# Output projection to feed-forward: new weight layout and order at the seam, and parts 2, 3, 3, 3 of the first down product

## The chip, the cores and the metric

The kernel runs on one core of a Trainium2 chip. Its engines are TensorE (PE: matmuls into the accumulator memory PSUM), VectorE (DVE), ScalarE (ACT) and GpSimd (POOL) for elementwise work, and SyncE (SP), whose queue issues all DMAs here. The on-chip memory is SBUF. The metric is the time of one execution on the device in microseconds, as the median of several runs.

## The reference

One encoder layer is applied to two sequences of 1024 tokens and 1024 channels, all in float32:

```python
h = rms_norm(x, ln_mix_pre); z = h @ w_in            # -> pool group | q | k | v
mix = jnp.concatenate([pool_out, attn_out], axis=-1) @ w_out
x = x + rms_norm(mix, ln_mix_post)
h = rms_norm(x, ln_ffn_pre)
f = (jax.nn.silu(h @ w_gate) * (h @ w_up)) @ w_down  # 1024 -> 2816 -> 1024
x = x + rms_norm(f, ln_ffn_post)
e = p @ w_ple_proj
g = jax.nn.sigmoid(x @ w_ple_gate + b_ple_gate)
return x + e * g
```

The change touches what lies between `@ w_out` and the first products of the feed-forward, and the order of the parts of `@ w_down` for the first sequence.

## The kernel before

A float32 product is done as three products of a rounded part ("hi") and a rest ("lo"): hi x hi, hi x lo, lo x hi. The hi of each operand is a copy on ScalarE, the lo a subtraction on VectorE. This making of two parts is called a split here.

**Output projection.** The mixed channels of 16 tiles of 128 tokens are multiplied by `w_out` (8 strips of 128 rows, split and resident in `wout_0` to `wout_3`, two strips in each). For each tile n: SP loads the mixed channels (`mixed_in`), ScalarE and VectorE split them into `ct` (`concat_hi`, `concat_lo`), TensorE multiplies two column halves one after the other (`mix_half`), 24 matmuls each. Then `post_a` (norm, gain, residual, giving `x1`), `turn_back` (TensorE transposes x1), `x1_out` (ScalarE copies it out of PSUM), `post_b` and `turn_scale` (the second norm's scale, transposed), GpSimd's gain (`xg`), and `h2_out` on VectorE, which writes `h2a` for an even and `h2b` for an odd tile. For each pair of tiles GpSimd makes four more operands from these (`forms_made`), and SP stores seven forms in memory (`store_forms`), and each tile's x1 (`store`).

**Feed-forward.** It is a blocked product of Strassen's kind: 7 products instead of 8 for a block of 2 x 2. A *unit* is one block of output; it has 7 *steps*, and step i multiplies form i of the activations (resident in `reg[:, k, i]`, k up to 4) with form i of the weights, which pass through the three places of `ring`. Steps are counted by `st`; UNITS holds all of them. Gate and up: 11 units j per sequence, nk = 4, that is 24 matmuls of 128 x 512 a step. Down: the inner dimension of 22 blocks is 11 pairs, cut into four parts by `DPART`; each part has two units q, and a step has 6 x nk matmuls: 18 for nk = 3, 12 for nk = 2. Parts after the first are added to `acc` (on VectorE and, for three of four blocks, on GpSimd: `add_base`). The last part's results leave through `ev` to `f_turned`.

Around each step, in the code's order: `weights_hi(st + 2)` on ScalarE, `weights_lo(st + 2)` on VectorE, the weight sums on GpSimd (`sums`), and the accumulations out of PSUM on VectorE (`g_tile`, `c22_middle`, `c22_end`, `c11_end`, `c12_end`, `c21_end`). Every engine works through its list strictly in order. TensorE's step st waits for `w_split` (the lo of its weights) and, in the first unit on new forms, for the form: for a gate product `op_split`, for a down product `op_in`.

**Filling `reg`.** The forms of a down part are loaded straight into `reg` (`fill_in`), form i when the last unit before has done its step i. For a gate product (`f` = 0 for sequence 0, 5 for sequence 1) 14 pieces of 1024 elements, two for each form, go through six places (three of `stg`, three of `fhi`): SP loads (`piece_in`), ScalarE copies (`fill_hi`), VectorE subtracts (`fill_lo`), and the place is free again (`stg_free`). For sequence 1 this is done in steps 3 to 6 of the last down unit and 0 to 2 of the next.

`reg` lies over the memory of the output projection (`wout`, `h2a`, `h2b`, `x1t`, `x1`, `xs_d`, `mixn`, `forms`). So a fill waits until what lay there is read: in `fill_hi` forms 0 to 3 wait for `mix_done` of the last tile, form 4 for the stores of even pairs, 5 and 6 for those of all pairs and of x1:

```python
elif i < 4:
    act.wait_ge(S["mix_done"], 2 * NSEQ * NT)
else:
    act.wait_ge(S["h2_st0"], 32 * NP * NSEQ)
    if i >= 5:
        act.wait_ge(S["h2_st1"], 32 * NP * NSEQ)
```

The order at the seam is that of the code: on TensorE lines L1332 to L1368, on SP the loop over n that ends in the pieces, on ScalarE and VectorE the loop over tiles, then `post_a(15)` and the fills, then the loop over steps.

Of the kernel before, what the change touches and what calls it, by code (L numbers as in the profile page):

```python
# [55 lines left out]
DPART = (3, 3, 3, 2)  # L56
DPART0 = (0, 3, 6, 9)
# [20 lines left out]
LASTP = len(DPART) - 1  # L78
# [110 lines left out]
def encoder_layer(nc, x, xt, p, ident_d, cos_d, sin_d, edge_d, g_mix_pre, g_mix_post, w_in, pool_w,  # L189
# [12 lines left out]
    with top:  # L202
# [26 lines left out]
        def stage_end(e):  # L229
# [65 lines left out]
        wout_0 = sb(s_d, "wout_0", [P, 2, 2, D], F32R)  # L295
        h2a = sb(s_d, "h2a", [P, 2, KT, P])
        x1t = sb(s_d, "x1t", [P, KT, P])
        wout_1 = sb(s_d, "wout_1", [P, 2, 2, D], F32R)
        h2b = sb(s_d, "h2b", [P, 2, KT, P])
        x1 = sb(s_d, "x1", [P, D])  # L300
        wout_2 = sb(s_d, "wout_2", [P, 2, 2, D], F32R)
        xs_d = sb(s_d, "xs_d", [P, 2, D])
        mixn = sb(s_d, "mixn", [P, D])
        wout_3 = sb(s_d, "wout_3", [P, 2, 2, D], F32R)
# [3 lines left out]
        gpost = sb(s_d, "gpost", [P, D])  # L308
        sb(s_d, "ws_ring_d", [P, 2 * 2 * CH + 3 * 4 * CH])
        ct_1 = sb(s_d, "ct_1", [P, 2, KT, P], F32R)  # L310
        gffn = sb(s_d, "gffn", [P, KT])
        rows_r = sb(s_d, "rows_r", [P, P])
        sb(s_d, "gffn_rest", [P, D - KT - P])
        junk_d = sb(s_d, "junk_d", [P, D], BF16)
        sb(s_d, "stg_d", [P, 3 * 2 * CH])
        xg = sb(s_d, "xg", [P, KT, P])
        s_d.close()
        wout, ct = (wout_0, wout_1, wout_2, wout_3), (ct_0, ct_1)
# [65 lines left out]
            "x1_sum", "x1_scale", "x1_root", "h2_ready", "x1_turned", "x1_out", "h2_turned", "h2_out", "x1_stored",  # L384
# [90 lines left out]
        def _(sp):  # L475
# [140 lines left out]
            def weights_in(u, m):  # L616
# [43 lines left out]
            def piece_in(f, q):  # L660
# [123 lines left out]

            for n in range(NSEQ * NT):
# [1666 lines left out]
```

## Time and profile before

| what | value |
|---|---|
| median of 3 runs | 2411.22 us (2408.73 to 2412.57) |
| profiled execution | 2405.9 us |
| its span | 2404.1 us |
| PE busy | 2332.2 us (97%) |
| DVE busy | 1688.6 us (70%) |
| ACT busy | 1046.8 us (44%) |
| POOL busy | 929.3 us (39%) |
| granted TensorE clock, mean | 0.989 |
| DMA | 394.30 MB, mean 164 GB/s |

Shares are of the span. A busy PE is not one at its peak, since the ends of its pipelined matmuls are modelled: what counts is the distance between starts. Idle time of an engine other than PE costs something only where PE ends up waiting for it. In rows of the trace the releaser of a wait stands behind `<-`, with the tile that it wrote and its line.

### The profile page before, as it was taken

The numbers are of one execution on the slowest core, as the hardware profiler recorded it, in microseconds if no ns is written. First come the engines' busy times: TensorE is split into PE (matmuls) and PEld (weight loads), VectorE is DVE, ScalarE is ACT, GpSimd is POOL, SyncE is SP. The second block draws the span as 40 slices with busy tenths as digits, with TensorE's granted clock in tenths as the row PEclk, the third lists the DMA queues.
The fourth block names the chain that finished last, engine by engine and source line by source line (L and its number), as shares of the span: only waits on it lengthen the run. The fifth ranks groups of instructions, "written<-read, shape, count | busy, mean of one in ns | idle before, by whom it ended". The sixth has DMA issues, their size and how long they took to land.

```text
span 2404.1 us, 29814 instructions
## 1 busy us (share of the span) xinstructions
PE 2332.2 (97%) x11120; PEld 1933.1 (80%) x11120; DVE 1688.6 (70%) x1785; ACT 1046.8 (44%) x1554; POOL 929.3 (39%) x557
## 2 busy tenths in 40 slices
PE   8999999999999979999999999899999999999999
PEld 7888788888777867888888888688788888877877
DVE  5756888888744667767666556888888866565752
ACT  4433788888743444333333222444433333233321
POOL 0000335444314554444444365454446634550210
PEclk9999999999999989999999999999999999999999
DMA  5222211100058785535447766655457596677431
GB/s 196 74 78 87 84 40 36 40 31 32 24 149 236 208 244 161 169 125 171 149 154 304 277 237 199 220 184 192 158 189 246 202 349 254 238 248 241 147 116 75
DMA packets 315103, 394.30 MB, mean 164 GB/s; under 512 B 18513, under 2 KB 222161, under 8 KB 314833
## 3 DMA queue, kind: packets, MB, share of 16 engines
q1 hardware_dynamic: 314960, 392.40, 48.4%
q8 instruction: 90, 1.47, 0.3%
q14 instruction: 53, 0.43, 0.1%
HBM read 254.99 MB, written 137.36 MB: 163 GB/s over the span
## 4 chain that ended last, share of the span: by engine, by line
PE 84%; DVE 8%; issue 3%; DMA 2%; ACT 2%; SPq 1%; POOL 1%; DVEq 0%; POOLq 0%; ACTq 0%
PE ps L1348 45%; PE ps L1126 32%; PE ps L1129 7%; DVE reg L2092 2%; DVE ring L2084 1%; DMA xb<-x_turned 1%; SPq L632 1%; DMA f_turned<-ev 1%; DVE fb L2393 0%; POOL fb L1120 0%; DVE x2l L2224 0%; DVE fhi L2203 0%; DVE rnorm L2390 0%; SPq L614 0%; DMA stg<-mix_turned 0%
## 5 line engine op out<-in xcount | busy, mean ns | idle before, releaser
L1348 PE MATMUL ps<-reg,ring 128*128 128x512 f32 x5544 | 1271.9, 392 | 28.7 <-DVE ring L2084 20.9
L1348 PEld LDWEIGHTS ps<-reg,ring 128*128 128x128 f32 x5544 | 1046.8, 189 | 253.2 <-DVE ring L2084 26.1
L1448 ACT ACTIVATE ring<-wraw 128x1024 fp32r<-128x1024 f32 (+2 forms) x152 | 143.7, 946 | 385.5 <-PE ps L1348 382.1
L2084 DVE TENSOR_TENSOR ring<-wraw,ring 128x1024 fp32r<-128x1024 f32 (+2 forms) x152 | 231.3, 1523 | 64.2 <-ACT ring L1448 63.3
L1126 PE MATMUL ps<-win,ht 128*128 128x512 f32 (+1 forms) x1152 | 227.2, 358 | 10.2 <-DVE win L1929 10.0
L1126 PEld LDWEIGHTS ps<-win,ht 128*128 128x128 f32 x1152 | 190.6, 191 | 40.6 <-issue 10.6
L1448 ACT ACTIVATE ring<-ws 128x1024 fp32r<-128x1024 f32 (+2 forms) x114 | 107.9, 947 | 237.0 <-PE ps L1348 228.7
L2028 DVE TENSOR_TENSOR pt<-ps,pt 128x512 fp32r<-128x512 f32 x256 | 173.0, 687 | 46.5 <-ACT pt L1448 42.3
L2084 DVE TENSOR_TENSOR ring<-ws,ring 128x1024 fp32r<-128x1024 f32 (+2 forms) x114 | 176.8, 1551 | 40.3 <-ACT ring L1448 39.1
L1126 PE MATMUL ps<-wout,ct 128*128 128x512 f32 x768 | 185.4, 401 | 7.0 <-DVE ct L2040 7.0
L1448 ACT ACTIVATE pt<-ps 128x512 fp32r<-128x512 f32 x256 | 153.7, 601 | 62.7 <-PE ps L1129 59.3
L1126 PEld LDWEIGHTS ps<-wout,ct 128*128 128x128 f32 x768 | 145.9, 193 | 38.3 <-DVE ct L2040 7.6
L1033 POOL TENSOR_TENSOR ws<-wraw,ws 128x1024 f32<-128x1024 f32 (+2 forms) x38 | 83.5, 2198 | 208.8 <-DMA wraw<-in_w_up 110.8
L1993 DVE TENSOR_REDUCE negmax<-ps 128x1 f32<-128x1024 f32 x128 | 156.0, 1219 | 9.8 <-PE ps L1126 8.6
L1129 PEld LDWEIGHTS ps<-ident,prob 128*128 128x128 f32 x1024 | 125.7, 140 | 42.5 <-issue 11.0
L1129 PE MATMUL ps<-ident,prob 128*128 128x128 f32 x1024 | 153.5, 272 | 2.4 <-DVE pt L2028 2.2
L1126 PE MATMUL ps<-keys,qs 128*128 128x512 f32 x512 | 150.8, 417 | 1.1 <-ACT prob L1564 1.1
L1126 PE MATMUL ps<-pt,values 128*128 128x512 f32 x512 | 149.8, 415 | 0.0
L1064 POOL TENSOR_TENSOR acc<-acc,ev 128x1024 f32<-128x1024 f32 x36 | 106.4, 2957 | 102.8 <-DVE ev L2104 102.8
L1564 ACT ACTIVATE prob<-ps,negmax 128x1024 f32<-128x1024 f32 x128 | 142.7, 1115 | 1.6 <-DVE negmax L1993 1.6
L1039 POOL TENSOR_TENSOR ws<-wraw,ws 128x1024 f32<-128x1024 f32 (+2 forms) x38 | 104.5, 2749 | 52.9 <-DVE ring L2084 52.9
L1027 POOL TENSOR_TENSOR ws<-wraw 128x1024 f32<-128x1024 f32 (+2 forms) x38 | 100.3, 2639 | 46.0 <-DVE ring L2084 46.0
(209 smaller groups left out, 2959.3 us busy)
## 6 DMA issues: line engine op xcount, KB each, us to landing
reg<-ff_forms SPq DMA_DIRECT2D x42, 1536.0 KB, 10.1
ff_forms<-fhi SPq DMA_DIRECT2D x88, 512.0 KB, 3.2
wraw<-in_w_gate SPq DMA_DIRECT2D x88, 256.0 KB, 4.2
wraw<-in_w_up SPq DMA_DIRECT2D x88, 256.0 KB, 4.6
ff_forms<-ev SPq DMA_DIRECT2D x44, 512.0 KB, 2.9
wraw<-in_w_down SPq DMA_DIRECT2D x48, 384.0 KB, 5.7
reg<-ff_forms SPq DMA_DIRECT2D x14, 1024.0 KB, 5.9
xt_a<-in_xt SPq DMA_DIRECT2D x16, 512.0 KB, 4.5
```

Of the source, the lines that this page charges most:

```text
L1027: ins = nc.gpsimd.tensor_tensor(s0, raw_block(u, 0, 0), raw_block(u, 1, 0), ALU.subtract)
L1033: ins = nc.gpsimd.tensor_tensor(s1, raw_block(u, 1, 1), s0, ALU.subtract)
L1039: ins = nc.gpsimd.tensor_tensor(s1, raw_block(u, 0, 1), s1, ALU.subtract)
L1064: nc.gpsimd.tensor_tensor(t, t, ev[:, 0], ALU.add).then_inc(S["acc_sum"], 1)
L1126: return nc.tensor.matmul(out, lhs, rhs, start=start, stop=stop)
L1129: return nc.tensor.transpose(out, src, ident[:])
L1348: last = nc.tensor.matmul(ps[:, 2 * chain + m, :], ring[:, st % 3, a, m, k * P:(k + 1) * P], reg[:, k, i, e, :], start=OPENS[i] and k == 0 ...
L1448: copy = lambda out, src, **k: nc.scalar.activation(out, src, ACT.Copy, **k)
L1564: nc.scalar.activation(prob[:, s % 2, :], pair(2 * (s % 2)), ACT.Exp, bias=negmax[:, s:s + 1], scale=1.0, accum_out=rowsum[:, s:s + 1]).th ...
L1993: V.tensor_reduce(negmax[:, s:s + 1], pair(2 * (s % 2)), AX.X, ALU.max, negate=True)\
L2028: V.tensor_tensor(pt[at][:, 1], ps[:, 4 + half, :].rearrange("p (k n) -> p k n", k=4), f(pt[at][:, 0]), ALU.subtract).then_inc(S["p_split" ...
L2084: V.tensor_tensor(ring_block(u, st, 1), weight_source(u, i), f(ring_block(u, st, 0)), ALU.subtract).then_inc(S["w_split"], 1)
```

## The change

1. `w_out` is laid by form: hi and lo of the strips are placed so that, after strips 3, 4 and 6 of the last tile, the memory of forms 0, 1 and 2 is free (`w_out_at`, semaphore `wout_free`). `gpost`, `gffn` and `rows_r` move, so that the place of piece 5 is free early.
2. TensorE runs the last tile strip by strip, both halves in each strip; `turn_scale(13)` stands after strip 3 and `turn_back(14)` after strip 5. Step 0 of the feed-forward follows at once, with `turn_scale(14)` in it, then `turn_back(15)`, step 1 with `turn_scale(15)`, step 2.
3. On ScalarE and VectorE forms 0 and 1 are filled ahead of `post_a(15)`.
4. SP: pieces 2 and 5 are loaded in the turn of tile 12, 0, 1, 3, 4 in that of tile 13, 6 to 9 in that of tile 15; pieces 10 to 13 stand ahead of the stores of the last pair. The first three weight halves are loaded one by one in the turns of tiles 4, 6 and 8, not all in that of tile 3.
5. Sequence 0's down product is cut into parts of 2, 3, 3, 3 pairs in place of 3, 3, 3, 2; sequence 1's stays.

```diff
-DPART = (3, 3, 3, 2)
-DPART0 = (0, 3, 6, 9)
+DPART = ((2, 3, 3, 3), (3, 3, 3, 2))
+DPART0 = ((0, 2, 5, 8), (0, 3, 6, 9))
...
+        def w_out_at(k, b):
+            at = 2 * k + b
+            if at < 4:
+                return wout_0[:, at]
+            form, row = divmod(at - 4, 3)
+            return (wout_1, wout_2, wout_3)[row][:, form]
+
+        WOUT_FREE = {3: 0, 4: 1, 6: 2}
...
-                elif q == 5:
-                    sp.wait_ge(S["mix_read"], NSEQ * NT)
-                elif q >= 3:
+                elif q in (3, 4):
                     sp.wait_ge(S["mix_done"], 2 * (NSEQ * NT - 1))
...
-                elif n == NSEQ * NT - 3:
+                if n == LAST - 3:
                     for b in range(2):
                         sp.wait_ge(S[f"h2_st{b}"], 16 * NP * 2)
+                    piece_in(0, 2)
+                    piece_in(0, 5)
+                if n == LAST - 2:
                     piece_in(0, 0)
...
+                if n == LAST:
+                    for q in range(6, 10):
+                        piece_in(0, q)
                 store(n)
-                if n == 3:
+                if n in (4, 6, 8):
                     sp.wait_ge(S["strip_split"], 2 * KT)
-                    for m in range(2):
-                        weights_in(UNITS[0], m)
-                    weights_in(UNITS[1], 0)
+                    weights_in(UNITS[n // 8], n // 2 % 2 if n < 8 else 0)
...
-            for q in range(8, 10):
+            for q in range(10, NP * len(fill_pieces(0))):
                 piece_in(0, q)
             store_forms(NT - 1)
-            for q in range(10, NP * len(fill_pieces(0))):
-                piece_in(0, q)
...
+            for k in range(KT):
+                for c in range(2):
+                    mix_strip(n, c, k)
+                if k == 3:
+                    turn_scale(n - 2)
+                if k == 5:
+                    turn_back(n - 1)
...
+            product(UNITS[0], 0, NSEQ * NT - 2)
             turn_back(NSEQ * NT - 1)
-            product(UNITS[0], 0, NSEQ * NT - 1)
             pe.wait_ge(S["mix_read"], NSEQ * NT)
-            product(UNITS[0], 1)
+            product(UNITS[0], 1, NSEQ * NT - 1)
             pe.wait_ge(S["x1_out"], NSEQ * NT)
+            product(UNITS[0], 2)
...
-                elif i < 4:
+                elif i < 3:
+                    act.wait_ge(S["wout_free"], i + 1)
+                elif i == 3:
                     act.wait_ge(S["mix_done"], 2 * NSEQ * NT)
...
             h2_out(NSEQ * NT - 3)
+            fill_lo(0, 0)
+            fill_lo(0, 1)
             post_a(NSEQ * NT - 1)
-            fill_lo(0, 0)
             h2_out(NSEQ * NT - 2)
             post_b(NSEQ * NT - 1)
-            fill_lo(0, 1)
             h2_out(NSEQ * NT - 1)
```

On TensorE, from the middle of tile 15 to the first steps, the order before was this (`wout,ct` are output matmuls, `reg,ring` those of the feed-forward, `x` the transpose of x1, `rows_r` that of the scale):

```order
L1129 MATMUL ps<-ident,rows_r 128x128
L1126 MATMUL ps<-wout,ct 128x512 x24
L1129 MATMUL ps<-ident,x 128x128 x8
L1129 MATMUL ps<-ident,rows_r 128x128
L1129 MATMUL ps<-ident,x 128x128 x8
L1348 MATMUL ps<-reg,ring 128x512 x12
L1129 MATMUL ps<-ident,rows_r 128x128
L1348 MATMUL ps<-reg,ring 128x512 x3504
```

and it is now, in the same stretch:

```order
L1138 MATMUL ps<-ident,rows_r 128x128
L1135 MATMUL ps<-wout,ct 128x512 x12
L1138 MATMUL ps<-ident,x 128x128 x8
L1135 MATMUL ps<-wout,ct 128x512 x12
L1368 MATMUL ps<-reg,ring 128x512 x12
L1138 MATMUL ps<-ident,rows_r 128x128
L1368 MATMUL ps<-reg,ring 128x512 x12
L1138 MATMUL ps<-ident,x 128x128 x8
L1368 MATMUL ps<-reg,ring 128x512 x12
L1138 MATMUL ps<-ident,rows_r 128x128
L1368 MATMUL ps<-reg,ring 128x512 x3480
```

The transpose of tile 14 went into tile 15, step 0 came ahead of the transpose of tile 15, and the last scale's transpose into step 1.

On VectorE, from `h2_out(13)` (`h2b`) on, before (`reg` rows are `fill_lo`, `ring` rows `weights_lo`, `mixn` and `x` belong to `post_a`):

```order
L2070 TENSOR_TENSOR h2b<-xg,ps 128x1024
L2046 RECIPROCAL small<-small 128x1
L2048 SCALAR_TENSOR_TENSOR mixn<-ps,small,gpost 128x1024
L2055 TENSOR_TENSOR x<-mixn,xs_d 128x1024
L2092 TENSOR_TENSOR reg<-stg,reg 128x2x512 x2
L2070 TENSOR_TENSOR h2a<-xg,ps 128x1024
L2059 RECIPROCAL small<-small 128x1
L2061 COPY rows_r<-small 128x128
L2092 TENSOR_TENSOR reg<-stg,reg 128x2x512
L2092 TENSOR_TENSOR reg<-fhi,reg 128x2x512
L2070 TENSOR_TENSOR h2b<-xg,ps 128x1024
L2092 TENSOR_TENSOR reg<-fhi,reg 128x2x512 x2
```

and now:

```order
L2095 TENSOR_TENSOR h2b<-xg,ps 128x1024
L2117 TENSOR_TENSOR reg<-stg,reg 128x2x512 x3
L2117 TENSOR_TENSOR reg<-fhi,reg 128x2x512
L2071 RECIPROCAL small<-small 128x1
L2073 SCALAR_TENSOR_TENSOR mixn<-ps,small,gpost 128x1024
L2080 TENSOR_TENSOR x<-mixn,xs_d 128x1024
L2095 TENSOR_TENSOR h2a<-xg,ps 128x1024
L2084 RECIPROCAL small<-small 128x1
L2086 COPY rows_r<-small 128x128
L2095 TENSOR_TENSOR h2b<-xg,ps 128x1024
L2117 TENSOR_TENSOR reg<-fhi,reg 128x2x512 x2
L2117 TENSOR_TENSOR reg<-stg,reg 128x2x512 x2
```

The four splits of forms 0 and 1 came ahead of the last tile's norm; forms 2 and 3 and the third weight split stay behind its `h2b`.

On SP, the last pieces and the stores of the last two pairs, before:

```order
L614 DMA h_forms<-h2a 128x4x128 x2
L614 DMA h_forms<-h2b 128x4x128
L614 DMA h_forms<-forms 128x4x128 x4
L675 DMA stg<-h_forms 128x1024
L675 DMA fhi<-h_forms 128x1024
L614 DMA h_forms<-h2a 128x4x128 x2
L614 DMA h_forms<-h2b 128x4x128
L614 DMA h_forms<-forms 128x4x128 x4
L675 DMA fhi<-h_forms 128x1024 x2
L675 DMA stg<-h_forms 128x1024 x2
```

and now:

```order
L627 DMA h_forms<-h2a 128x4x128 x2
L627 DMA h_forms<-h2b 128x4x128
L627 DMA h_forms<-forms 128x4x128 x4
L686 DMA fhi<-h_forms 128x1024 x2
L686 DMA stg<-h_forms 128x1024 x2
L627 DMA h_forms<-h2a 128x4x128 x2
L627 DMA h_forms<-h2b 128x4x128
L627 DMA h_forms<-forms 128x4x128 x4
```

The last four pieces stand ahead of the last pair's seven stores.

## Rows read from the trace of the kernel before

**Rows 1.** Whom TensorE waited for, whole span: us in total, times, longest.

```profile
PE ps L1348 <- DVE ring L2084: 20.9, 11, 5.8
```

**Rows 2.** TensorE in order of time: start, us, instruction, count [idle before].

```profile
745.80 5.70 PE L1126 MATMUL ps<-wout,ct 128*128 128x512 f32 x24
...
755.71 8.48 PE L1126 MATMUL ps<-wout,ct 128*128 128x512 f32 x24 [3.33 <-DVE ct L2040]
```

**Rows 3.** The same view of TensorE, at the seam.

```profile
865.23 1.03 PE L1129 MATMUL ps<-ident,x 128*128 128x128 f32 x8
...
871.72 1.94 PE L1129 MATMUL ps<-ident,x 128*128 128x128 f32 x8 [5.34 <-DVE x L2055]
876.28 5.22 PE L1348 MATMUL ps<-reg,ring 128*128 128x512 f32 x12 [2.63 <-issue]
...
893.93 12.74 PE L1348 MATMUL ps<-reg,ring 128*128 128x512 f32 x48 [4.15 <-issue]
910.00 15.27 PE L1348 MATMUL ps<-reg,ring 128*128 128x512 f32 x66 [3.33 <-DVE ring L2084]
```

**Rows 4.** TensorE in order of time, end of sequence 0.

```profile
1505.46 11.17 PE L1348 MATMUL ps<-reg,ring 128*128 128x512 f32 x48 [1.63 <-DVE ring L2084]
1522.42 4.78 PE L1348 MATMUL ps<-reg,ring 128*128 128x512 f32 x12 [5.79 <-DVE ring L2084]
1529.81 12.71 PE L1348 MATMUL ps<-reg,ring 128*128 128x512 f32 x48 [2.61 <-DVE ring L2084]
```

**Rows 5.** Whom TensorE waited for, 1480 to 1560.

```profile
PE ps L1348 <- DVE ring L2084: 12.0, 6, 5.8
```

**Rows 6.** SP's DMA issues in order of time, early output tiles.

```profile
730.27 0.67 SPq L632 DMA_DIRECT2D wraw<-in_w_gate  x1
...
747.00 0.87 SPq L557 DMA_DIRECT2D stg<-mix_turned  x1
```

**Rows 7.** ScalarE in order of time, the same stretch.

```profile
753.34 1.06 ACT L1448 ACTIVATE ct<-stg 128x1024 fp32r<-128x1024 f32 x1 [10.47 <-DMA stg<-mix_turned]
```

**Rows 8.** ScalarE in order of time, at the seam.

```profile
903.58 2.25 ACT L1448 ACTIVATE reg<-fhi 128x1024 fp32r<-128x1024 f32 x2 [9.58 <-DMA fhi<-h_forms]
```

**Rows 9.** VectorE in order of time, at the seam.

```profile
868.69 0.16 DVE L2046 RECIPROCAL small<-small 128x1 f32<-128x1 f32 x1 [5.96 <-ACT small L1452]
...
871.54 4.50 DVE L2092 TENSOR_TENSOR reg<-stg,reg 128x1024 fp32r<-128x1024 f32 x2
...
882.48 1.22 DVE L2070 TENSOR_TENSOR h2b<-xg,ps 128x1024 f32<-128x1024 f32 x1 [0.34 <-DVE reg L2092]
...
891.75 1.97 DVE L2084 TENSOR_TENSOR ring<-wraw,ring 128x1024 fp32r<-128x1024 f32 x1 [0.24 <-DVE reg L2092]
```

**Rows 10.** SP's DMA issues, at the seam.

```profile
894.25 3.47 SPq L614 DMA_DIRECT2D h_forms<-forms  x4
```

**Rows 11.** VectorE in order of time, end of sequence 0.

```profile
1512.87 6.73 DVE L2092 TENSOR_TENSOR reg<-stg,reg 128x1024 fp32r<-128x1024 f32 x2
...
1522.29 3.40 DVE L2092 TENSOR_TENSOR reg<-stg,reg 128x1024 fp32r<-128x1024 f32 x1
...
1534.88 4.56 DVE L2092 TENSOR_TENSOR reg<-stg,reg 128x1024 fp32r<-128x1024 f32 x2
1541.58 1.22 DVE L2171 TENSOR_TENSOR ev<-acc,ps 128x1024 f32<-128x1024 f32 x1 [2.13 <-DMA f_turned<-ev]
```

**Rows 12.** VectorE in order of time, start of the first down product.

```profile
1307.47 1.22 DVE L2171 TENSOR_TENSOR ev<-ev,ps 128x1024 f32<-128x1024 f32 x1 [2.75 <-PE ps L1348]
...
1317.49 2.03 DVE L2203 TENSOR_TENSOR fhi<-ev,fhi 128x1024 fp32r<-128x1024 f32 x1 [0.75 <-DMA ff_forms<-fhi]
...
1321.91 0.95 DVE L2084 TENSOR_TENSOR ring<-wraw,ring 128x768 fp32r<-128x768 f32 x1
```

**Rows 13.** Busy time by stretch; at the end granted clock, DMA share, GB/s.

```profile
1307.00:1312.00 5.00, 5.00 (x23) 4.14 (x23) 4.53 (x5) 3.77 (x5) 3.43 (x4) 1.00 1.03 410
1452.00:1458.00 6.00, 6.00 (x28) 4.95 (x27) 1.32 (x2) 1.76 (x2) 0.00 (x0) 1.00 0.69 218
```

More of the change, by code:

```diff
@@ L68, in ffn_units @@
             out.append(Unit(len(out), s, False, j, 0, 0, KG, 5 * s))
-        for part in range(len(DPART)):
+        for part in range(len(DPART[s])):
             for q in range(2):
-                out.append(Unit(len(out), s, True, 0, part, q, DPART[part], 5 * s + 1 + part))
+                out.append(Unit(len(out), s, True, 0, part, q, DPART[s][part], 5 * s + 1 + part))
     return out
@@ L77 @@
 NST = NU * NP
-LASTP = len(DPART) - 1
+LASTP = len(DPART[0]) - 1
 FIRST_OF = {u.fill: u.n for u in reversed(UNITS)}
@@ L294, in encoder_layer @@
         s_d = ExitStack()
-        wout_0 = sb(s_d, "wout_0", [P, 2, 2, D], F32R)
+        wout_0 = sb(s_d, "wout_0", [P, 4, D], F32R)
         h2a = sb(s_d, "h2a", [P, 2, KT, P])
         x1t = sb(s_d, "x1t", [P, KT, P])
-        wout_1 = sb(s_d, "wout_1", [P, 2, 2, D], F32R)
+        wout_1 = sb(s_d, "wout_1", [P, 4, D], F32R)
         h2b = sb(s_d, "h2b", [P, 2, KT, P])
         x1 = sb(s_d, "x1", [P, D])
-        wout_2 = sb(s_d, "wout_2", [P, 2, 2, D], F32R)
+        wout_2 = sb(s_d, "wout_2", [P, 4, D], F32R)
         xs_d = sb(s_d, "xs_d", [P, 2, D])
         mixn = sb(s_d, "mixn", [P, D])
-        wout_3 = sb(s_d, "wout_3", [P, 2, 2, D], F32R)
+        wout_3 = sb(s_d, "wout_3", [P, 4, D], F32R)
         forms = sb(s_d, "forms", [P, 2, 4, KG, P])
@@ L316, in encoder_layer @@
         xg = sb(s_d, "xg", [P, KT, P])
+        gffn = sb(s_d, "gffn", [P, KT])
+        rows_r = sb(s_d, "rows_r", [P, P])
         s_d.close()
-        wout, ct = (wout_0, wout_1, wout_2, wout_3), (ct_0, ct_1)
+        ct = (ct_0, ct_1)
+        def w_out_at(k, b):
[5 more added lines that the diff above has]
+        WOUT_FREE = {3: 0, 4: 1, 6: 2}
         two = ExitStack()
@@ L624, in weights_in @@
                     if u.down:
-                        r0, c0 = (NJ * m + DPART0[u.part]) * P, (KG * nh + 2 * u.q) * P
+                        r0, c0 = (NJ * m + DPART0[u.seq][u.part]) * P, (KG * nh + 2 * u.q) * P
                         sp.dma_start(down_view(u, m)[:, nh, 0:u.nk].rearrange("p k x n -> p k (x n)"),
@@ L650, in fill_in @@
                 if part:
-                    k0, nk = DPART0[part - 1], DPART[part - 1]
+                    k0, nk = DPART0[s][part - 1], DPART[s][part - 1]
                     sp.wait_ge(S["step_done"], NP * (FIRST_OF[f] - 1) + i + 1)
@@ L680, in forms_landed @@
                 s, part = divmod(f, 5)
-                pairs = DPART0[part - 1] + DPART[part - 1]
+                pairs = DPART0[s][part - 1] + DPART[s][part - 1]
                 for k in (1, 2):
@@ L783, in norm_in @@
                         sp.dma_start(x2_d[0, :, n, :], stg[:, (POST_X2 + 2 * n) % 3, :]).then_inc(S["x2_out"], 16)
+            LAST = NSEQ * NT - 1
             for n in range(NSEQ * NT):
@@ L1298, in mix_strip @@
                     last.then_inc(S["mix_done"], 1)
+                elif n == NSEQ * NT - 1 and c == 1 and k in WOUT_FREE:
+                    last.then_inc(S["wout_free"], 1)
             def mix_half(n, c):
@@ L1325, in _ @@
                     mix_strip(0, c, k)
-            for n in range(1, NSEQ * NT):
+            for n in range(1, NSEQ * NT - 1):
                 mix_half(n, 0)
@@ L1331, in _ @@
                 turn_back(n - 1)
-            turn_scale(NSEQ * NT - 2)
+            n = NSEQ * NT - 1
+            pe.wait_ge(S["c_split"], n + 1)
+            pe.wait_ge(S["mix_read"], n - 1)
+            for k in range(KT):
[5 more added lines that the diff above has]
+                    turn_back(n - 1)
             def product(u, i, between=None):
@@ L1376, in _ @@
                         pe.wait_ge(S["sum_root"], 1)
-                    if u.n or i >= 2:
+                    if u.n or i >= 3:
                         product(u, i)
@@ L1595, in out_strip @@
                 act.wait_ge(S[f"strip_in{k}"], 32)
-                copy(wout[k // 2][:, 0, k % 2], out_place(k)).then_inc(S["strip_hi"], 1)
+                copy(w_out_at(k, 0), out_place(k)).then_inc(S["strip_hi"], 1)
             q_out(0, 0)
@@ L1768, in _ @@
                     post_b(n - 1)
+                    if n == NSEQ * NT - 1:
+                        fill_hi(0, 0)
                     x1_out(n - 1)
```

27 lines of the change are left out of this document (10 added, 17 removed).

## The prediction

> **What bounds the kernel now.** TensorE is busy for 2332.2 of 2404.1 us, so only the places where it stands still or runs at the lower clock can give time back. I read first who TensorE waited for over the whole span [rows 1]: the longest in total is the weight split of the feed-forward products, 20.9 us in 11 waits. Then TensorE's instructions in order of time, for where they lie. Three places come out.
>
> Place A, early in the output product [rows 2]: a wait of 3.33 us, after which 24 matmuls take 8.48 us, where the undisturbed 24 take 5.70. Their starts lie 0.35 us apart on average instead of 0.23, so part of them ran at the lower of the clock's two levels (1.2, not 2.4 GHz): 2.78 us more. A costs 6.1 us.
>
> Place B, the seam between output product and feed-forward [rows 3]: the last output matmuls end at about 866, and from 910.00 on TensorE runs with no wait. Between them it does 4 steps of 24 matmuls; at 11.17 us for 48, 0.2327 each, at full clock [rows 4] those are 22.3 us, the transposes some 2. So about 20 of 44 us are lost, to waits of 5.34, 2.63, 4.15 and 3.33 and to the lower clock (12 matmuls in 5.22, 48 in 12.74 instead of 11.17).
>
> Place C, the end of sequence 0's down product and the start of sequence 1 [rows 4]: 12.0 us of waits in 6 [rows 5], and the lower clock makes 12 matmuls 4.78 (2.9 at full clock) and 48 matmuls 12.71, that is 1.9 + 1.5 more. C costs 15.4 us.
>
> **The change, place A.** SP issues the first three weight halves in one piece, 12 DMAs from 730.27, then the form stores, and only at 747.00 the tile that ScalarE needs [rows 6]; ScalarE idles 10.47 us for it and splits it at 753.34 [rows 7], 10.5 late against the 11.9 us beat of the tiles. Afterwards 4 DMAs stand behind the stores of tiles 4, 6 and 8, which carry no form stores. SP issued 19 DMAs from 730.27 to 747.00, 0.88 us each; four are 3.5 us. The form stores of an odd tile, 7 DMAs, are longer than that and stay, so no tile load comes later than those behind form stores do already. I take all 6.1 us. Bounds: 0 (three small stalls in place of one) to 6.1; if only the wait goes and a slow stretch stays, 3.3.
>
> **Place B, step by step, on the clock of the trace before.** What moves: the last tile runs strip by strip for both halves, the transpose of tile 14 goes into it, and the splits of forms 0 and 1 come ahead of the last tile's norm, since a form's place is free after strips 3, 4, 6.
> 1. Tile 15 starts at 854.1 (two halves of 5.55 before the transpose at 865.23). Strips 0 to 3 are 24 matmuls, 5.7 us: form 0 is free at 859.9. ScalarE is through with tile 14's second norm at about 861.1 and copies form 0's two pieces by 863.3 (2.25 for two by [rows 8]).
> 2. VectorE is idle for 5.96 us, from 862.7 to 868.69, before the last tile's first norm, and the splits begin behind it at 871.54 [rows 9]. The two splits go there, about 1.2 to 2.3 each: form 0 ready at 866.1. TensorE ends tile 15 at about 866.0 with the transpose in it. Step 0 starts at 866.2 instead of 876.28, at full clock, and ends at 872.1.
> 3. Form 1 (4.5, the price of two splits at 871.54) keeps VectorE until 870.8, then the last norm takes 3: the last rows are ready at 873.9, not 871.6. TensorE waits 1.8 us for them, transposes, does step 1 and is done at 880.5.
> 4. Step 2 needs the third weight split, which stands on VectorE behind h2b of tile 15 and forms 2 and 3. h2b needs the scale transpose, which now lies in the middle of step 1 (877.8), so VectorE stands 2.4 us before it: h2b until 879.6, four pieces until 887.7, the weight split 1.97 (at 891.75 now) [rows 9]: 889.7. So of the 10 us won at step 0, only 893.93 - 889.8 = 4.1 are left at step 2; the rest has become a wait of 9.3 us in front of it.
> 5. Step 4 is set by another chain. ScalarE holds form 5 until the forms of the last pair are stored, since it overwrites them. SP issued these 7 stores until 897.72 (the last four of them in [rows 10]) and then the pieces, which came in at 903.58 [rows 8]. Now the last four pieces go first, in the time when SP waits for the last pair anyway. GpSimd makes the last pair after h2b, which comes at 878.4 instead of 882.48 [rows 9]: 4.1 us sooner, stores from 889.0 to 894.5 behind the pieces, landed about 898.3. ScalarE begins 5.3 us sooner and VectorE's split for step 4 ends at 904.4. By the matmuls: 889.8 + 12.74 = 902.5, with a colder start 903.8. The later decides: 904.4 instead of 910.00. Gain 5.6 us, the same for all that follows. Bounds: 0 (the store of the last pair lands as late as now) to 8 (its chain follows the 10 us of step 0 almost whole).
>
> **Place C and the order 2, 3, 3, 3.** The same matmuls are done, but the part with 12 matmuls a step (2.79 us) goes from the end of sequence 0 to its beginning; at the end stand steps of 18 (4.19). The next sequence's forms are split in steps 3 to 6 of the last unit and 0 to 2 of the next: 6.73, 3.40 + 1.22, 2.59, 4.56 us and so on, with the accumulations and weight splits between [rows 11]. VectorE is busy there nearly throughout, 47.7 us against 4 x 2.79 + 3 x 5.58 = 27.9 us of matmuls. With 18 a step it is 33.5 us. Counted from step 2 of the last unit (0): the first two splits end at 14.6, the split for step 6 at 17.3 (due 16.75: wait 0.6), that for the next unit's step 0 at 24.6 (due 21.5: wait 3.1), step 1 on time; then VectorE waits until 1541.58 [rows 11] for a store of ev that SP issues behind the pieces; in the new count it lands at 36.2, step 2 starts at 38.7 (due 35.8: wait 2.9), step 4 on time. Sum 6.6, and once the lower clock, 1.6. The 15.4 become 8.2: gain 7.2. Bounds: 3 (the waits only move) to 13.
>
> The other end pays. From the end of the last gate unit (1307.47) the left-over of that unit holds VectorE to 1319.5, and the fifth weight split is made at 1321.91 to 1322.86 [rows 12]; with 18 matmuls a step it is due at 1307.4 + 16.8 = 1324.2, with 12 at 1318.6. The load of forms is smaller in front of it (2 of 3 pairs; the DMA engines are full there, 410 GB/s [rows 13]), so the store that ScalarE waits for lands sooner; I count the weight splits at two thirds and one contended split less, and get 1320.5: a new wait of 1.9 us. Bounds: 0 to 5 (4.3 by the unchanged times, and some clock).
>
> On the contention: the same split of 1024 elements took 3.36 each at 1512.87 and 2.25 at 871.54, while the sum that reads PSUM took 1.22 at 1541.58 [rows 9, 11]. At 1.22 for every split of C the sum would be the second rival's. The Trainium skill (GPSIMD Engine Reference, section Specifications) says that GpSimd shares its SBUF interfaces with VectorE and that VectorE instructions with two SBUF inputs contend; these rows agree, and the change doesn't take the sums of GpSimd away from the last unit.
>
> **Sum.** 6.1 + 5.6 + 7.2 - 1.9 = 17.0 us. The profiled execution took 2405.9 us (span 2404.1), 5.3 below the median of 2411.22; I take the gain off the median: 2394.2.
>
> **Rivals.**
> 1. Part of it is given back: the wait in front of step 2 runs colder than I count, or C's waits only move (3 instead of 7.2), or a small stall stays in A (3.3). For it: VectorE's work is the same, and SP is near its limit on odd tiles. Two of the three: 17.0 - 4.2 - 2.8 = 10, 2401.
> 2. More: in the longer last unit the splits meet less of GpSimd's sums (three accumulations and three weight sums, done 19 us after step 2 begins). At 1.22 a split, C loses nothing: 15.4 instead of 7.2, 25.2 in all, 2386. Against it: these sums start with the unit, as the splits do.
> 3. Slower: the forms of part 1 (7 loads of 128 x 3 x 2 x 512 values, 1.57 MB each, and 1.6 MB of weights, 12.6 MB) must now come in beside the short unit of part 0, between its first step and step 6 of part 1: 6 x 2.79 + 6 x 4.19 = 41.9 us, where they had 12 x 4.19 = 50.3. It decides from 12.6/41.9 = 300 GB/s down. Full engines give 410, 31 us; the same stream between 1452 and 1458 ran at 218 GB/s [rows 13]: 58 us, a stall of 16. With that, 5 at the beginning of the part, C lost in it and A and B worth 7 together: 2411.2 + 16 + 5 - 7 = 2425. Against it: at 1452 SP issued a load only per finished step, so 218 is the pace of TensorE, not a limit.
> 4. The seam doesn't move, since the last pair's stores decide and are not sooner (B 0), and the new wait is 5: 6.1 + 7.2 - 5 = 8.3, 2403; it lies within the first one's reach.
>
> **Chances.** My forecast (13 to 21 us less) 0.48; the first and the fourth together 0.30; the second 0.12; little or nothing left, 0 to 5 less, 0.06; slower 0.04. A change under 0.2%, 4.8 us, can't be told from none here. Faster 0.90, same 0.06, slower 0.04. The range leaves out half of the second and the last two: 2386 to 2405.
>
> **What would show it.** A: no wait of TensorE before tile 7, all tiles 11.9 us apart. B: step 0 within 1 us of the last output matmul, a wait of about 9 us before step 2, ended by the weight split, and step 4 some 38 us after the end of tile 15 (now 44). C: waits of at most 3 us each, the largest before the next unit's step 0 and step 2. A wait of about 2 us at step 4 of the first down unit. If the first down product shows loads as what TensorE waits for, the third rival holds; if C's total stays above 10 us, VectorE's work and not the length of the steps decides there.

## The result, and the profile after

| | before | after |
|---|---|---|
| median | 2411.22 us (2408.73 to 2413.70, 5 runs) | 2398.55 us (2397.93 to 2399.13, 5 runs) |
| profiled execution | 2405.9 us | 2398.45 us |
| its span | 2404.1 us | 2396.7 us |
| PE busy | 2332.2 us | 2325.9 us |
| granted clock, mean | 0.989 | 0.991 |

The ratio is 0.9946, 95% interval 0.9933 to 0.996: 12.7 us less, where 17.0 were forecast. The time lies in the range (2386 to 2405). The two spans differ by only 7.4 us, since the profiled execution of before was 5.3 under its median, so places are compared below by distances within a trace, and sizes by the medians.

Whom TensorE waited for over the whole span, after (us in total, times, longest), answers to [rows 1]:

```profile
PE ps L1368 <- DVE ring L2109: 30.7, 11, 9.0
...
PE ps L1135 <- DVE ct L2065: 3.6, 1, 3.6
```

The wait for weight splits has grown from 20.9 to 30.7 us in a kernel that is faster. The releaser's name misleads: at the seam VectorE itself waited for other things, as will be seen. The wait for `ct` that made place A is gone.

TensorE after, in order of time (start, us, instruction, count, idle before): the first output matmul, place A, and the seam, answering to [rows 2, 3].

```profile
667.46 24.34 PE L1135 MATMUL ps<-wout,ct 128*128 128x512 f32 x96 [3.64 <-DVE ct L2065]
...
751.97 5.70 PE L1135 MATMUL ps<-wout,ct 128*128 128x512 f32 x24
...
763.87 5.70 PE L1135 MATMUL ps<-wout,ct 128*128 128x512 f32 x24
...
856.76 2.98 PE L1135 MATMUL ps<-wout,ct 128*128 128x512 f32 x12
859.58 2.89 PE L1368 MATMUL ps<-reg,ring 128*128 128x512 f32 x12
...
862.33 2.98 PE L1368 MATMUL ps<-reg,ring 128*128 128x512 f32 x12
867.50 1.09 PE L1138 MATMUL ps<-ident,x 128*128 128x128 f32 x8 [2.19 <-DVE x L2080]
868.35 3.00 PE L1368 MATMUL ps<-reg,ring 128*128 128x512 f32 x12
...
883.15 13.14 PE L1368 MATMUL ps<-reg,ring 128*128 128x512 f32 x48 [8.96 <-DVE ring L2109]
...
902.22 13.13 PE L1368 MATMUL ps<-reg,ring 128*128 128x512 f32 x45 [5.92 <-DVE ring L2109]
```

Tiles are 11.9 us apart with no slow stretch: A is gone. Step 0 stands 2.82 us behind the start of the last 12 output matmuls, with no gap. The wait before step 2 is 8.96 us (9.3 forecast). But a second one of 5.92 us stands before step 4, longer than the 3.33 that stood there before. From the first output matmul to step 4 it is 902.22 - 667.46 = 234.8 us; before it was 242.7 (the same wait for `ct` started that stage at 667.29). That is 7.9 less, A and seam together, where 11.7 were forecast. Two things lie outside this distance. Behind the wait of 5.92 us the first 45 matmuls take 13.13 us, where 45 at full clock take 10.5 (0.2327 each): 2.7 us more, which the 66 behind [rows 3]'s last wait did not lose. So at a later point, VectorE's split of 3.41 us in the gate product (1203.81 before, 1198.63 after), only 5.4 us of the 7.9 are left. And from the first output matmul to the wait-free stretch behind place C (1555.46 before, 1546.62 after) it is 9.0 us less: that is the whole gain that this pair of traces shows.

SP's DMA issues after, at the seam (start, us that the issuing took, queue, transfer, count), answering to [rows 10], and ScalarE in the same stretch, to [rows 8]:

```profile
876.15 3.10 SPq L627 DMA_DIRECT2D h_forms<-forms  x4
879.29 1.61 SPq L686 DMA_DIRECT2D fhi<-h_forms  x2
880.95 0.93 SPq L686 DMA_DIRECT2D stg<-h_forms  x2
881.99 1.78 SPq L627 DMA_DIRECT2D h_forms<-h2a  x2
883.81 2.69 SPq L627 DMA_DIRECT2D h_forms<-h2b  x1
886.55 4.64 SPq L627 DMA_DIRECT2D h_forms<-forms  x4
```

```profile
895.80 2.00 ACT L1470 ACTIVATE reg<-fhi 128x1024 fp32r<-128x1024 f32 x2 [9.39 <-DMA h_forms<-forms]
```

VectorE has been idle since 889.2; what is late is form 5, which ScalarE may not write before the last pair's stores have read `forms`. The seven stores took 9.2 us to issue, from 881.99 to 891.19. How full the DMA engines are at that time the table of busy time by stretch shows (the last three numbers are the granted clock, the DMA share and GB/s):

```profile
876.00:882.00 6.00, 0.00 (x0) 0.00 (x0) 5.37 (x4) 0.00 (x0) 5.64 (x4) 0.59 1.18 346
882.00:888.00 6.00, 4.85 (x13) 3.87 (x14) 4.11 (x4) 2.95 (x3) 3.29 (x1) 0.55 0.98 317
888.00:894.00 6.00, 6.00 (x28) 4.96 (x27) 1.20 (x1) 0.00 (x0) 2.38 (x1) 1.00 1.09 335
```

The share is at or above 0.98 from the pieces' loads on until 894; ScalarE goes on at 895.80. The engines have next to nothing to spare in between.

The first down product, TensorE and then VectorE after; the latter answers to [rows 12]:

```profile
1315.95 9.43 PE L1368 MATMUL ps<-reg,ring 128*128 128x512 f32 x33 [2.80 <-DVE ring L2109]
```

```profile
1310.51 2.31 DVE L2228 TENSOR_TENSOR fhi<-ev,fhi 128x1024 fp32r<-128x1024 f32 x1
1314.07 1.22 DVE L2129 TENSOR_TENSOR ev<-ev,ps 128x1024 f32<-128x1024 f32 x1 [1.25 <-ACT ev L1470]
1315.21 0.68 DVE L2109 TENSOR_TENSOR ring<-wraw,ring 128x512 fp32r<-128x512 f32 x1
```

ScalarE's copy out of PSUM (the `ev` that VectorE waits for) came at 1313.01, behind the split `fhi` of the left-over gate unit, then the accumulation, then the weight split of 0.68 us. The wait is 2.80 us, and the 33 matmuls behind it take 9.43 instead of 7.7 (33 x 0.2327): some 1.7 us of lower clock more.

End of sequence 0, TensorE after, answering to [rows 4]; below it the same stretch's waits, to [rows 5]:

```profile
1513.54 4.42 PE L1368 MATMUL ps<-reg,ring 128*128 128x512 f32 x18 [1.16 <-DVE ring L2109]
1520.97 12.79 PE L1368 MATMUL ps<-reg,ring 128*128 128x512 f32 x48 [3.01 <-DVE ring L2109]
1535.14 11.17 PE L1368 MATMUL ps<-reg,ring 128*128 128x512 f32 x48 [1.38 <-DVE ring L2109]
1546.62 13.67 PE L1368 MATMUL ps<-reg,ring 128*128 128x512 f32 x59 [0.30 <-DVE ring L2109]
```

```profile
PE ps L1368 <- DVE ring L2109: 5.9, 4, 3.0
```

The 12.0 us of waits have become 5.9 (6.6 forecast), and the lower clock costs 12.79 - 11.17 = 1.6 and some 0.2 in the 18, in place of 3.4.

### The profile page after: what moved, and what is told of

It is laid out like the page before. It is cut to its first block, busy times and chain, and to the rows that moved or that the text cites. A ratio compares the mean times of both kernels' runs of the same rounds, so it can differ in the third digit from the quotient of the medians.

```text
span 2396.7 us, 29816 instructions
## 1 busy us (share of the span) xinstructions
PE 2325.9 (97%) x11120; PEld 1928.8 (80%) x11120; DVE 1681.0 (70%) x1785; ACT 1045.1 (44%) x1554; POOL 935.9 (39%) x557
## 4 chain that ended last, share of the span: by engine, by line
PE 84%; DVE 7%; issue 3%; DMA 2%; ACT 2%; POOL 2%; SPq 1%; DVEq 0%; POOLq 0%; ACTq 0%
PE ps L1368 45%; PE ps L1135 32%; PE ps L1138 7%; DVE ring L2109 1%; DVE reg L2117 1%; DMA xb<-x_turned 1%; DMA f_turned<-ev 1%; DVE ev L2228 0%; DVE fhi L2228 0%; POOL fb L1129 0%; DVE fb L2418 0%; SPq L627 0%; DVE x2l L2249 0%; DVE rnorm L2415 0%; DMA stg<-f_turned 0%
## 5 line engine op out<-in xcount | busy, mean ns | idle before, releaser
L1368 PE MATMUL ps<-reg,ring 128*128 128x512 f32 x5544 | 1271.2, 391 | 31.6 <-DVE ring L2109 30.7
L2109 DVE TENSOR_TENSOR ring<-ws,ring 128x1024 fp32r<-128x1024 f32 (+2 forms) x114 | 171.8, 1507 | 42.5 <-ACT ring L1470 41.4
## 6 DMA issues: line engine op xcount, KB each, us to landing
reg<-ff_forms SPq DMA_DIRECT2D x42, 1536.0 KB, 10.1
```

Source lines behind the costliest of these rows:

```text
L1368: last = nc.tensor.matmul(ps[:, 2 * chain + m, :], ring[:, st % 3, a, m, k * P:(k + 1) * P], reg[:, k, i, e, :], start=OPENS[i] and k == 0 ...
L2109: V.tensor_tensor(ring_block(u, st, 1), weight_source(u, i), f(ring_block(u, st, 0)), ALU.subtract).then_inc(S["w_split"], 1)
```

## The experiments

All were timed in five rounds beside the kernel before, whose median was 2410.83 us in the first four, 2410.76 in the next four and 2409.94 in the last three. Two theories stand behind them. The first: the change is a sum of three independent gains and one price, and the seam gave little since the loads of pieces 10 to 13 (the four pieces, 512 KB each) fill the DMA engines ahead of the last pair's stores. The rival: the places are one chain (what is won early is given back late), or the seam is held by VectorE's work.

### The changed kernel again

> The changed kernel again, beside its parts. Both theories: 2398 to 2400 us, some 12 below the kernel before.

2399.35 us (2398.47 to 2400.43), ratio 0.9951 (0.9938 to 0.9963): 11.5 less. The first output matmul came at 669.54 and step 4 at 904.54, 235.0 apart, with waits of 2.19, 8.62 and 4.54. The seven stores were issued in 7.9 us here, from 886.01 to 893.87, and behind the last wait 39 matmuls took 10.68 us (9.1 at full clock). From the first output matmul to behind C this execution is 10.1 us shorter than that of before. Against this run the later ones are set; the kernel before, timed beside each group, differs by 0.9 us at most between the groups.

### The weights' loads alone

```diff
-                if n == 3:
+                if n in (4, 6, 8):
                     sp.wait_ge(S["strip_split"], 2 * KT)
-                    for m in range(2):
-                        weights_in(UNITS[0], m)
-                    weights_in(UNITS[1], 0)
+                    weights_in(UNITS[n // 8], n // 2 % 2 if n < 8 else 0)
```

> The kernel before with only the weight loads spread over tiles 4, 6 and 8. If the load of tile 7 behind 12 weight DMAs and 7 form stores is all of place A: no wait before tile 7, tile 14 begins 6.5 us sooner, the seam and the rest as before, 6.5 us less in all. If the seam depends on the weights' timing too, its waits (5.34, 2.63, 4.15, 3.33) change.

2405.18 us (2402.27 to 2407.07), ratio 0.9976 (0.9967 to 0.9986): 5.65 less, where the term for A was 6.1 and 6.5 were expected here. Tile 15's second half starts 6.8 us sooner than before (at 853.63 for 859.69, the first output matmul at 668.00 for 667.29), and from the first output matmul to step 4 it took 236.7 us, 6.0 less than before. The code of its seam is the old one, but its waits are not quite the old ones:

```profile
865.65 1.94 PE L1127 MATMUL ps<-ident,x 128*128 128x128 f32 x8 [5.34 <-DVE x L2053]
870.22 4.84 PE L1346 MATMUL ps<-reg,ring 128*128 128x512 f32 x12 [2.63 <-issue]
...
887.86 12.76 PE L1346 MATMUL ps<-reg,ring 128*128 128x512 f32 x48 [4.51 <-issue]
904.71 10.53 PE L1346 MATMUL ps<-reg,ring 128*128 128x512 f32 x38 [4.09 <-DVE ring L2082]
```

The last two waits are 8.6 us together, where they were 7.5 before, and the 38 matmuls behind them take 10.53 instead of 8.8. At the split of 3.41 us in the gate product (1200.11) the trace is only 4.4 us ahead. The next two runs form such a pair too, with the old loads and with the new ones, and show 4.0. So in the traces part of what A wins is given back at the old seam, as the rival said of such gains; the medians, over 10 and 17 executions, give 5.65. Why the traces show less stays open, but the profiled execution of before was itself some 5 us under its median.

### The parts 2, 3, 3, 3 alone

```diff
-DPART = (3, 3, 3, 2)
-DPART0 = (0, 3, 6, 9)
+DPART = ((2, 3, 3, 3), (3, 3, 3, 2))
+DPART0 = ((0, 2, 5, 8), (0, 3, 6, 9))
```

> The kernel before with only the parts 2, 3, 3, 3 for sequence 0. Place C gives 7.8 us and the start of the first down product costs 4.1 (2.8 of wait, the rest lower clock): 3.7 us less. The rival, that the new wait comes from the sooner seam and is not there with the old one, gives 7.8 less.

2406.02 us (2402.87 to 2409.27), ratio 0.998 (0.997 to 0.999): 4.8 less, which is C less its price D (3.7 were expected, 7.8 by the rival). The wait at the start of the down product is there in this kernel too, 2.81 us at 1321.68, so the sooner seam didn't bring it; those of C are 1.14, 3.03, 1.09 and 0.27.

### Both, with the old seam

The kernel before with the two edits above.

> Both of these together, with the old seam. If the new seam gives nothing (my reading of the trace after: 2.2 + 9.0 + 5.9 us of waits and two cold starts against 5.3 + 2.6 + 4.2 + 3.3), this is as fast as the changed kernel or up to 1.5 us faster. If the seam gave what was forecast (5.6), it is 5.6 us slower than the changed kernel.

2400.54 us (2399.19 to 2401.59), ratio 0.9954 (0.9942 to 0.9967): 10.3 less, against 5.65 + 4.8 = 10.4 for the two by themselves. They add up, as closely as intervals of 2 to 3 us either way can tell. What is left for the whole new seam is 11.5 - 10.3 = 1.2 us, which by these medians alone is not clear of nothing (2399.19 to 2401.59 here, 2398.47 to 2400.43 with the new seam). The traces show 236.8 us from the first output matmul to step 4 with the old seam, 235.0 and 234.8 with the new one, and at the split of 3.41 us 1.9 and 1.1 less.

### Why the seam gives so little: pieces of an eighth

This kernel leaves out seven eighths of the values of forms 5 and 6, so it doesn't compute the layer; it is there for its times.

```diff
+                cols = CH // 8 if f == 0 and q >= 10 else CH
-                sp.dma_start(fill_slot(q).rearrange("p (k n) -> p k n", n=CH), h2f_d[...])
+                sp.dma_start(fill_slot(q).rearrange("p (k n) -> p k n", n=CH)[:, :, 0:cols], h2f_d[..., 0:cols])
```

> The changed kernel with an eighth of the data in the loads of pieces 10 to 13 (forms 5 and 6 get the rest of their values from what lay there). If the volume of these four loads (2.1 MB) is what made the seven stores of the last pair slow to issue (9.2 us in place of the 5.5 that I counted) and late to land, the stores are issued in 5 to 6 us and land 3 to 4 us sooner, and step 4 starts 3 to 4 us sooner. If SP is slowed by something else (the number of DMAs, what stands before them), nothing moves.

2392.41 us (2391.62 to 2393.13), ratio 0.9923 (0.9911 to 0.9936), 6.9 less than the changed kernel. SP's issues of the last stores, and TensorE at step 4:

```profile
885.85 0.91 SPq L627 DMA_DIRECT2D h_forms<-h2a  x2
886.80 0.56 SPq L627 DMA_DIRECT2D h_forms<-h2b  x1
887.41 3.54 SPq L627 DMA_DIRECT2D h_forms<-forms  x4
```

```profile
900.79 9.59 PE L1370 MATMUL ps<-reg,ring 128*128 128x512 f32 x41 [0.97 <-DVE ring L2111]
```

The same seven stores are issued in 5.1 us instead of the 9.2 and 7.9 in the two traces of the changed kernel, and step 4 comes 231.3 us after the first output matmul, 3.7 sooner than in the changed kernel. Number and place of the four loads in SP's list are unchanged, so their volume made the stores late. Of the 6.9 us not all belongs to this: the trace has 3.7 to step 4, 1.6 for the slow stretch behind it, which is gone, and 1.6 at the first down product, where the same wait of 2.81 us is there but no slow stretch followed it (858 matmuls in 194.77 us, 196.40 in the changed kernel). The edit doesn't touch that place.

### The last pair's stores ahead of the pieces

```diff
+            store_forms(NT - 1)
             for q in range(10, NP * len(fill_pieces(0))):
                 piece_in(0, q)
-            store_forms(NT - 1)
```

> The changed kernel with the last pair's seven stores ahead of pieces 10 to 13, as before. If the pieces ahead only take DMA time from the stores: the stores land 4 us sooner, the pieces come last and decide, so form 5 starts at about the same time, within 1.5 us. If the order was worth the 5 us counted in the forecast, this is 4 to 5 us slower.

2394.97 us (2392.76 to 2398.54), ratio 0.9937 (0.9924 to 0.9949), 4.4 less than the changed kernel. Neither expectation came: form 5 was expected at about the same time, or the whole slower. SP, and TensorE at step 4:

```profile
882.80 0.91 SPq L627 DMA_DIRECT2D h_forms<-h2a  x2
883.75 0.57 SPq L627 DMA_DIRECT2D h_forms<-h2b  x1
884.37 3.46 SPq L627 DMA_DIRECT2D h_forms<-forms  x4
887.87 1.68 SPq L686 DMA_DIRECT2D fhi<-h_forms  x2
```

```profile
900.26 5.98 PE L1368 MATMUL ps<-reg,ring 128*128 128x512 f32 x25 [3.02 <-DVE ring L2109]
```

Step 4 comes after 232.2 us instead of 235.0, and the 25 matmuls behind the wait run at full clock (25 x 0.2327 = 5.8), where the 39 behind the wait of 4.54 in the changed kernel took 10.68 instead of 9.1: 2.8 + 1.6 = 4.4. ScalarE now waits until 893.84 for the pieces themselves, not for the stores. That is 225.8 us after the first output matmul, 2.8 sooner than in the changed kernel (898.12 - 669.54 = 228.6): the eleven transfers are issued in 7.7 us from 882.80, where the other order took 12.0 (881.87 to 893.87), although it began sooner. "Pieces ahead of last stores" is a part of the change that costs time.

### Forms 5 and 6 one step later

```diff
                     m = st + 4 - NP * FIRST_OF[f]
+                    if f == 0 and m >= 5:
+                        m = 5 if m == 6 else 6 if m == 7 else NP
                     if 0 <= m < NP:
```

In both loops over steps, ScalarE's and VectorE's, so that the weights of step 4 are split before form 5 is waited for.

> The changed kernel; ScalarE and VectorE fill forms 5 and 6 of the first gate unit one step later, behind the weight split of steps 4 and 5. If step 4 waits only since its weight split is queued behind form 5, which waits for the last pair's stores: step 4 follows step 3 with no or little wait (896.3 in place of 902.2), step 5 has its form by 900, and the whole is 5 to 6 us faster. If something else holds step 4 (its own weights, the accumulation before it), the wait of 4.5 to 5.9 us stays.

2395.07 us (2392.71 to 2396.94), ratio 0.9936 (0.9922 to 0.9949), 4.3 less than the changed kernel, where 5 to 6 were expected.

```profile
883.92 18.67 PE L1368 MATMUL ps<-reg,ring 128*128 128x512 f32 x72 [8.95 <-DVE ring L2111]
902.79 5.74 PE L1368 MATMUL ps<-reg,ring 128*128 128x512 f32 x24 [0.21 <-DVE ring L2111]
910.60 9.63 PE L1368 MATMUL ps<-reg,ring 128*128 128x512 f32 x41 [2.07 <-DVE ring L2111]
```

Steps 2 to 4 run through, and a smaller wait of 2.07 us has come before step 6. So the weight split of step 4 was late because form 5 stood ahead of it on ScalarE and VectorE.

### The short part second: 3, 2, 3, 3

```diff
-DPART = ((2, 3, 3, 3), (3, 3, 3, 2))
-DPART0 = ((0, 2, 5, 8), (0, 3, 6, 9))
+DPART = ((3, 2, 3, 3), (3, 3, 3, 2))
+DPART0 = ((0, 3, 5, 8), (0, 3, 6, 9))
```

> The changed kernel with parts 3, 2, 3, 3 for sequence 0: the short part second. If the wait at step 4 of the first down unit (2.8 us and 1.3 of lower clock) comes from the gate unit's left-over work meeting short steps, it is gone, and the whole is 4 us faster. The rival: the short second part brings GpSimd's and VectorE's additions into steps of 2.7 us and loads beside them, as the last part did before, and loses as much or more there.

2394.7 us (2391.89 to 2394.86), ratio 0.993 (0.9917 to 0.9942), 4.6 less than the changed kernel. In the first down units only this is left:

```profile
1371.97 8.25 PE L1368 MATMUL ps<-reg,ring 128*128 128x512 f32 x35 [0.24 <-DVE ring L2109]
```

The waits of C are as before this edit: 1.14, 3.03, 1.15, 0.29. So D cost 4.5 to 4.6 us (2.8 of wait and 1.7 of clock in the trace), and C's gain does not depend on it.

### Two and three of them together

The edits above combined, without new code.

> The changed kernel with two edits: parts 3, 2, 3, 3 for the first sequence, and the last pair's seven stores ahead of pieces 10 to 13. Alone they gave 4.6 and 4.4 us at places 450 us apart. Theory (losses at separate places add): 2399.35 - 4.6 - 4.4 = 2390.3 us, within 1.5. Rival (each is partly the same recovery, for instance of the clock, or a stall elsewhere takes it back): 2394 or more. In the trace the theory wants step 4 about 232 us after the first output matmul, and no wait of more than 0.5 us in the first down unit.

2393.46 us (2391.60 to 2396.75), ratio 0.9932 (0.992 to 0.9945). By the medians that is 5.9 under the changed kernel, 3.2 us short of the sum and outside the 1.5 that the theory allowed. The trace sides with the sum: from the first output matmul to the first wait of C it is 1504.87 - 668.05 = 836.8 us; in the changed kernel 1514.74 - 669.54 = 845.2. 8.4 less, of 9.0 expected (the two edits alone: 840.8 and 840.5). The runs of this kernel lie 5 us apart, so the medians don't settle it. From C's first wait to the end it is 884.9 us, against 883.9 in the changed kernel and 883.6 to 884.8 in the other runs on it: at most a little was lost there, and the rest stays open.

> The changed kernel with parts 3, 2, 3, 3 and the late fills, stores behind the pieces as in the change. Theory (adding up): 2399.35 - 4.6 - 4.3 = 2390.4. Rival: 2394 or more. Against the run with all three this tells what the order of stores and pieces is still worth once the fills are late: the theory says 1 to 3 us (the 2.07 before step 6), the rival nothing.

2391.04 us (2389.80 to 2392.68), ratio 0.992 (0.9907 to 0.9934), 0.6 from the sum.

> The same, and forms 5 and 6 copied and split one step later, behind the weight split of the next step. Theory (stores first and late fills take away the same wait, the one before step 4, whose 3.0 us are left with the stores first): at most 3.0 and 1 of clock on top, less the new wait of 2.1 before the unit's step 6 that the late fills had, which goes as well if the stores land 3 us sooner: 2386.5 to 2389. Rival (fills that late only move the wait to step 5 or 6): 2390 to 2392, as without them. In the trace: no wait from step 2 to step 4, and the one before step 6 under 1 us or about 2.

2387.57 us (2386.43 to 2393.10, 4 runs), ratio 0.9912 (0.9898 to 0.9925): 22.4 us less than before, where the change alone gave 11.5 in its rounds. It is the fastest version.

```profile
883.75 36.52 PE L1368 MATMUL ps<-reg,ring 128*128 128x512 f32 x153 [8.96 <-DVE ring L2111]
...
1364.55 35.70 PE L1368 MATMUL ps<-reg,ring 128*128 128x512 f32 x156 [0.24 <-DVE ring L2111]
```

From step 2 on TensorE runs without a wait until 1364.55. The order of stores and pieces is still worth 3.5 us by the medians with late fills (2391.04 to 2387.57); with the stores behind the pieces a wait of 2.07 us still stands before step 6, with the stores first it is gone. The wait of 8.96 us before step 2 is the largest left at the seam; no run here changed what sets it.

## Why the prediction was right, and where it was not

| term | forecast | by medians | in the traces |
|---|---|---|---|
| A | 6.1 | 5.65 | 6.0 to step 4, 4.0 to 4.4 behind it |
| B | 5.6 | 1.2 | 1.8 to step 4, 1.1 and 1.9 behind it |
| C | 7.2 | 9.4 (4.8 + 4.6) | 7.7 |
| D | -1.9 | -4.6 | -4.5 |
| sum | 17.0 | 11.7 (11.5 and 12.7 measured) | 9.0 and 10.1 from first output matmul to behind C |

The median for C is not a measurement of C by itself: it is the gain of the parts alone, plus what the short part second gave back.

**A** held at its place. The load of three weight halves in one piece cost a wait and a slow stretch, and four DMAs at a time cost nothing: the tiles stay 11.9 us apart, and tile 15 comes 6.7 us sooner. Beyond the old seam the traces show less of it, as said above; the forecast had taken for granted that what is won at A stays won.

**B, steps 1 to 4** held on their clock: step 0 follows the output matmuls at once, TensorE waits 2.19 us for the last norm (1.8), then 8.96 for the third weight split (9.3). VectorE ends that split at 883.05; shifted by what A gave (5.9, as in the next paragraph), that is 889.0, where 889.7 was forecast. The 48 matmuls behind the wait take 13.14 us, 0.4 more than the 12.74 that the forecast had.

**B, step 5** failed: "stores from 889.0 to 894.5 behind the pieces, landed about 898.3". On the forecast's clock, which lacks A's 6.1 us and starts 0.2 earlier, the measured times are: stores issued from 887.9 to 897.1, ScalarE on form 5 at 901.7, step 4 at 908.2 instead of 904.4. The beginning came 1 us sooner than I thought; the issuing took 9.2 us where I had let 5.5 stand (in the second execution it began 0.9 us later than forecast and took 7.9, with nearly the same end: 897.7 on this clock). In the kernel before these stores took 5.1 us (892.67 to 897.72), but there no 2 MB of loads stood right ahead; [rows 13] showed that loads can fill the engines. Step 4 is 3.8 us late by this, and 4.4 us are missing in B. The forecast also counted no slow stretch behind step 4; 2.7 and 1.6 us were lost there. The traces with the old seam and the new loads lose 1.7 there too, so against them it is not a loss of the new seam. The Trainium skill (DMA: Bandwidth & Descriptors, section Queues, rings and completion order) says that on each DMA engine descriptors of one ring are consumed in order; the two runs with thin pieces and with the stores first agree: 5.1 and 5.0 us of issuing in place of 9.2, and ScalarE goes on at form 5 4.3 and 2.8 us sooner than in the second execution. Why full engines also slow the issuing itself no run shows. The fourth rival had the mechanism ("the last pair's stores decide and are not sooner"), though not all of its size.

**C** held in its sum: waits of 5.9 for a forecast 6.6. By place it was 1.16 before step 6 of the last unit (0.6 forecast), 3.01 before the next unit's step 0 (3.1), 1.38 before its step 2 (2.9) and 0.30 before its step 4 (none). Step 2 began 14.2 us behind step 0, and 14.1 were forecast (24.6 to 38.7): the store of `ev` lets VectorE go on at 1532.73, 11.8 us behind step 0 (11.6). But steps 0 and 1 took 12.79 us at the lower clock, and this shortened the wait behind them. The forecast had added 1.6 us of lower clock to a wait of 2.9 that already held it; with 0.5 too little for step 6 and 0.3 for step 4 the sum came out near. The second rival's uncontended splits did not come: two splits took 6.77 us at 1503.63 and one 3.43 at 1513.41, as in [rows 11].

**D** had the right place and the wrong size, for two reasons: the wait was 2.80 where I had 1.9, and I had counted no lower clock behind it, 1.7 us. I had applied the clock's price once in C and not here, though a wait of 2.61 in [rows 4] had been followed by such a slow stretch (12.71 for 48). That price doesn't always come: with thin pieces the same wait had none.

The third rival (loads of part 1) did not appear: nothing in the first down product waits for a load. The first rival's time, 2401, is near the result, but not by its mechanisms: nothing was left in A, and C's waits shrank. The time stayed in the range because the range left 11 us of room above the forecast: B fell short by 4.4 and D by 2.7 (by the medians), and C gave back between 0.5 (traces) and 2.2. The whole is 4.3 us short of the forecast (5.5 in the second measurement): the time in the range is partly luck, since two terms missed one way and one the other. One sign that the forecast had named was missed: step 4 some 38 us after the end of tile 15; it came 42.6 us after (859.6 to 902.22).

## What to carry to other kernels

Work that must land soon goes ahead of bulk transfers that can wait, even if the engine that issues them would otherwise stand idle for a microsecond or three: at a DMA share near 1, stores behind 2 MB of loads let ScalarE go on 2.8 us later here than stores ahead of them. Before moving a transfer forward, price what stands behind it at the rate of the full engines, and before shortening one step, see whether another chain (here the release of memory by a store) sets the next one. A short block of work belongs where the other engines have nothing left over from the block before: second, here, neither first nor last. And a gain at one place is measured again behind the next wait: of 6.8 us won at tile 15, the traces with the old seam kept 4.0 to 4.4.

## What was not expected of the hardware

- The time to issue grew when the DMA engines were full. Seven stores of 256 KB took 9.2 us at a DMA share of 0.98 to 1.18 (7.9 in the second execution), and 5.0 to 5.1 us when they went first or the loads before them were thin. Behind the pieces even the two for `h2a` took 1.78 us (1.46), and 0.91 in those two runs.
- A wait of TensorE of about 3 us doesn't always cost clock. Behind 2.80 and 3.01 us (at 1315.95 and 1520.97) 1.7 and 1.6 us were lost; behind 3.02 us at the seam in the run with the stores first nothing was, nor behind 2.81 us at the first down product in the run with thin pieces. After the same wait of 2.19 us the 8 transposes took 1.09 us in one execution of the changed kernel and 1.91 in another. What decides it these runs don't show; a forecast has to carry 0 to 1.7 us for each such wait.
- Removing a wait of 2.81 us gave 4.6 us, and one edit that moved step 4 by 2.8 us gave 4.4: the clock returned over half of the wait itself.
